# The first column pair of each MLP with seven products, its token sums made in the projection before it

## The reference

```python
def sq_relu_mlp(h, w_up, w_down):            # w_up 2048 x 8192, w_down 8192 x 2048, fp32
    return jnp.square(jax.nn.relu(h @ w_up)) @ w_down
...
h = h + sq_relu_mlp(rms_norm(h, mlp_norm_w[l]), w_up[l], w_down[l])
```

## Time and profile before

| | |
|---|---|
| median of 3 runs | 2415.95 us |
| profiled execution, device time | 2416.47 us |
| its span, first to last instruction | 2414.7 us |
| PE busy | 2404.3 us, 11523 matmuls |
| PEld / DVE / ACT / POOL busy | 2004.6 / 1935.6 / 1284.7 / 259.9 us |
| 16 DMA engines, mean | 222 GB/s |

### The profile page before, as it was taken

How to read it: one execution, slowest core, us unless ns; L and a number is a source line. 1 busy time by engine, 2 the same in 40 slices (tenths; PEclk the granted TensorE clock), 3 DMA queues, 4 the chain that set the end, 5 groups by cost and what they waited for, 6 DMA issues and landing times.

```text
span 2414.7 us, 31286 instructions
## 1 busy us (share of the span) xinstructions
PE 2404.3 (100%) x11523; PEld 2004.6 (83%) x11523; DVE 1935.6 (80%) x2107; ACT 1284.7 (53%) x1544; POOL 259.9 (11%) x394
## 2 busy tenths in 40 slices
PE   8999999999999999999999999999999999999999
PEld 7888888888888888888888888888888888888887
DVE  6788888875579889888899866566689898898897
ACT  5555565554455445455555645555555555454453
POOL 1011111111001001011011111110211010010010
PEclk9999999999999999999999999999999999999999
DMA  7777777767778668577677765655887676677684
GB/s 227 217 227 227 226 232 223 230 216 236 220 236 257 213 209 267 172 241 236 197 252 228 238 207 186 189 173 181 259 257 218 219 239 215 225 235 223 195 256 162
DMA packets 288110, 535.35 MB, mean 222 GB/s; under 512 B 22318, under 2 KB 55440, under 8 KB 286976
## 3 DMA queue, kind: packets, MB, share of 16 engines
q1 hardware_dynamic: 264736, 457.87, 59.9%
q0 software_dynamic: 22976, 75.91, 10.9%
q10 hardware_dynamic: 288, 0.11, 0.0%
HBM read 498.09 MB, written 35.72 MB: 221 GB/s over the span
## 4 chain that ended last, share of the span: by engine, by line
PE 67%; issue 25%; DMA 5%; POOL 2%; DVE 2%; ACT 0%; POOLq 0%; ACTq 0%
PE acc L515 9%; PE acc L517 9%; PE acc L516 9%; PE acc L693 7%; PE acc L695 7%; PE acc L694 7%; DMA spread<-work 4%; PE aux L515 2%; PE aux L516 2%; PE aux L517 2%; POOL work L2039 2%; PE aux L532 1%; PE aux L531 1%; PE aux L530 1%; PE aux L719 1%
## 5 line engine op out<-in xcount | busy, mean ns | idle before, releaser
L1085 ACT ACTIVATE w_hi<-w_raw 128x1024 fp32r<-128x1024 f32 x392 | 414.9, 1061 | 494.0 <-PE acc L695 379.6
L1303 DVE TENSOR_TENSOR w_lo<-w_raw,w_hi 128x1024 fp32r<-128x1024 f32 x353 | 427.8, 1221 | 236.8 <-ACT w_hi L894 236.5
L693 PE MATMUL acc<-w_hi,stationary 128*128 128x512 f32 x1564 | 609.9, 390 | 0.0
L694 PE MATMUL acc<-w_lo,stationary 128*128 128x512 f32 x1564 | 609.1, 389 | 0.0
L695 PE MATMUL acc<-w_hi,stationary 128*128 128x512 f32 x1564 | 609.1, 389 | 0.0
L1609 DVE TENSOR_TENSOR w_lo<-w_raw,w_hi 128x1024 fp32r<-128x1024 f32 x392 | 476.3, 1220 | 126.5 <-ACT w_hi L1085 121.0
L894 ACT ACTIVATE w_hi<-w_raw 128x1024 fp32r<-128x1024 f32 x353 | 370.2, 1057 | 299.2 <-PE acc L517 142.4
L515 PE MATMUL acc<-w_hi,stationary 128*128 128x512 f32 x960 | 379.8, 396 | 0.0
L517 PE MATMUL acc<-w_hi,stationary 128*128 128x512 f32 x960 | 374.4, 390 | 0.0
L516 PE MATMUL acc<-w_lo,stationary 128*128 128x512 f32 x960 | 374.2, 390 | 0.0
L693 PEld LDWEIGHTS acc<-w_hi,stationary 128*128 128x128 f32 x1564 | 293.6, 188 | 63.2 <-DVE w_lo L1609 2.9
(11 more groups left out here) (246 smaller groups left out, 2874.0 us busy)
## 6 DMA issues: line engine op xcount, KB each, us to landing
w_raw<-in_w_up SPq DMA_DIRECT2D x200, 512.0 KB
w_raw<-in_w_down SPq DMA_DIRECT2D x192, 512.0 KB
w_raw<-in_ssm_w_in SPq DMA_DIRECT2D x129, 512.0 KB
w_raw<-in_ssm_w_out SPq DMA_DIRECT2D x64, 512.0 KB
work<-in_w_down SPq DMA_DIRECT2D x64, 512.0 KB
w_raw<-in_w_kv SPq DMA_DIRECT2D x64, 512.0 KB
work<-in_w_up SPq DMA_DIRECT2D x56, 512.0 KB
spread<-work POOLq DMA_DIRECT2D x44, 512.0 KB, 4.8
```

The costliest lines, as they stand in the source:

```text
L693: pe.matmul(o, xh, hi[:, k], start=starts[t] and k == 0, stop=False)
L694: pe.matmul(o, xh, lo[:, k], start=False, stop=False)
L1085: a.activation(whi[:, unit % RING, :], raw[:, slot, :], ACT.Copy).then_inc(sem("hi_made"), 1)
L1303: v.tensor_tensor(wlo[:, s, :], raw[:, pos.raw_slot(off), :], whi[:, s, :].bitcast(F32), ALU.subtract).then_inc(sem("lo_made"), 1)
```

## The change

The first pair of each MLP becomes a form pair like the others, 19 units, with `w_up`'s quad moved from the k-tiles 12 to 15 to the k-tiles 0 to 3 (`UP_QUAD = 0`), so that the token sums come from block 0 of the residual and are made in the projection before. Its direct units go in an order that asks for the later k-tiles last (`late`). The quad's four pieces are loaded during the projection (`first_quad`). In the second pair, ACT's `fresh_relu` and DVE's `fresh_square` make way for the `add_half` and `square` of the other pairs; both halves are taken there (after units 1 and 3). The last product block of `ssm_w_out` takes its k-tiles in another order, which frees the place of the sums early. In layer 1 the PSUM banks of the forms change places, since the projection's last block stands in the other bank.

```diff
-UP_QUAD, DOWN_QUAD = 3, 0
+UP_QUAD, DOWN_QUAD = 0, 0
...
-FRESH_UNITS = ([("d", n, k) for n in (0, 1) for k in range(0, 12, 2)] + [("d", n, k) for n in (0, 1) for k in (12, 14)])
+FRESH_UNITS = pair_units(UP_QUAD, True)
...
-             + [(n, k) for n in (2, 3) for k in range(0, 32, 2)])
+             + [(2, k) for k in range(0, 32, 2)] + [(3, k % 32) for k in range(16, 48, 2)])
...
@@ SP: loads
+                if i in (56, 58, 60, 62):
+                    if i == 56:
+                        sp.wait_ge(sem("gate_lo"), GROUPS)
+                    first_quad(0, (1, 0, 3, 2)[(i - 56) // 2])
...
+                if i in (24, 26, 28, 30):
+                    if i == 24:
+                        sp.wait_ge(sem("o_ready"), 4)
+                    first_quad(1, (1, 0, 3, 2)[(i - 24) // 2])
...
@@ PE, mlp
                                 if formed(c, p) == 0:
-                                    pe.wait_ge(sem("resid_added"), R)
+                                    pe.wait_ge(sem("resid_added"), R - 1)
+                                    pe.wait_ge(sem("turned_lo"), T - 3)
+                            if what == "P7" and formed(c, p) == 0:
+                                pe.wait_ge(sem("resid_added"), R)
                             if what == "P5":
-                                if p == 1 and c == 0:
+                                if p == 0 and c == 0:
                                     pe.wait_ge(sem("sums_lo"), 5 * layer + 1)
...
@@ ACT, projections
+                if i == 57:
+                    a.wait_ge(sem("w_used"), Pos(OUT0).done(53))
+                    sums_hi(0, 0, 1, sums[1])
...
+                if i == 30:
+                    sums_hi(1, 0, 1, sums[1])
...
@@ ACT, mlp
-                                if j == 10:
+                                if j == 14:
                                     resid_hi(3, T, before)
-                                if j == 12:
-                                    sums_hi(0, 1, sums[1])
-                                continue
...
-                                if late and j in (1, 3):
-                                    fresh_relu(j // 2)
...
@@ DVE, projections
+                if i == 55:
+                    resid_sums(3, T_OUT + 1)
+                if i == 59:
+                    sums_lo(0, 0, 1, sums[1])
...
+                if i == 29:
+                    resid_sums(11, T_WO + 1)
+                if i == 31:
+                    sums_lo(1, 0, 1, sums[1])
...
@@ DVE, mlp
-                                if j == 10:
+                                if j == 14:
                                     resid_lo(3, T, before)
-                                if j == 11:
-                                    v.wait_ge(sem("turned_lo"), T)
-                                    resid_sums()
-                                if j == 13:
-                                    sums_lo(0, 1, sums[1])
-                                continue
...
                                 if late and j in (1, 3):
-                                    fresh_square(j // 2)
+                                    add_half(layer, j // 2, start - 3 + j)
+                                    square(c, j // 2)
                                     turn_up(c, j // 2)
```

117 lines of the change are left out of this document (54 added, 63 removed).

## The result

The changed kernel takes 2421.43 us in the median of 21 runs (2419.84 to 2424.35), the kernel before 2416.72 us in 21 runs beside it (2415.84 to 2418.88). The ratio is 1.0019 with a 95% interval of 1.0012 to 1.0026: slower by 4.7 us, where 3.5 were forecast, and within 0.2% of no change. The profiled execution took 2421.18 us of device time.

A forecast was written before the change was run, and what follows sets the result against it. PE, 100% busy, was taken to bound the kernel, with DVE's queue next. The terms -2.72 + 4.16 + 2.05 gave +3.49 us, 2419.4 us; range 2418.3 to 2420.9 around the forecast alone, 2415.6 to 2422.6 over all cases with exclusions.

The forecast's parts named there:

- term 2: First pair of MLP 1: DVE's chain from `w_o` makes unit 1 0.31 us and P7 1.74 us late, together +2.05 us.
- term 1: Second pair of each MLP: two added `add_half` make P7's split late, 2.08 us each, together +4.16 us.
- The saving: First pair of each MLP: twelve fewer matmuls in all at 0.2267 us each, -2.72 us.
- 1.27 us at the earliest: PE waiting for DVE: a matmul starts no sooner than 1.27 us after the start of its split.
- DVE has no pause here: Second pair of MLP 0: from the first `fresh_square` at 717.62 DVE's rows follow one another up to P7.
- DVE catches up and I count no further wait: Second pairs behind P7: one split per 2.04 us of PE at 1.13 us each, so no further wait.
- The price of `add_half`: DVE, second pairs: 1.26 us each as a dependent step; by the skill 1.13, making the whole change +2.97 us.
- the transfers in `w_o`: Bound on the sum: quad pieces loaded between the projection's pieces cost from nothing up.
- late pieces: Rival, `w_o`: quad loads delay its pieces by up to 6.2 us; half of that gives +6.6, 2422.5 us; chance 0.17.
- The first pair of MLP 0: P7's matmul at 684.14, due at 684.52: no wait, with 0.38 us to spare.
- only the second pairs wait: Rival: the chain through ACT is shorter, so MLP 1's first pair doesn't wait; +1.44, 2417.4 us; chance 0.14.
- Hidden: Rival: DVE's added work costs PE nothing, leaving only the saving; -2.72, 2413.2 us; chance 0.08.

The follow-up runs named there:

- the run with 8 columns: The changed kernel with the two added `add_half` of each second pair made on 8 of 512 columns: 2417.36 us against 2416.40, ratio 1.0001.
- the run with the second half later: The changed kernel with each second pair's second `add_half`, `square` and transpose moved from position 3 to 5, dependent work one or two positions back: 2419.44 us, ratio 1.0013.
- both queue remedies: The changed kernel with layer 1's quad loads ten pieces earlier (alone 2419.44 us) and `sums_hi` behind `resid_hi` (alone 2419.79 us); both together 2417.96 us.
- the first four experiments: Changed kernel with quad loads early, 2419.44 us; kernel before with the changed kernel's quad loads, 2417.41; changed kernel with `sums_hi` behind `resid_hi`, 2419.79; with both remedies, 2417.96.

## Why the prediction came out as it did

- **The number** lies in the whole range stated, 2415.6 to 2422.6, but 0.5 us above 2418.3 to 2420.9, the range around the forecast alone. Of the 2.0 us above 2419.4, 0.77 are the kernel before, whose median of 21 runs is higher than that of three. The other 1.2 are term 2, 1.60 too small, term 1, 0.86 too large, and the 0.5 that stands in no changed place. That two errors pull against each other is luck.
- **The saving** was right: 12 matmuls at an unchanged pitch of 0.2267 us. Every sum of the table starts from it.
- **Term 1**, the second pairs: place and mechanism were right, shown by the run with 8 columns. Its size was 2.08 us each and measured 1.65. The term that was mis-sized is the queue ahead of P7: I priced only the rows that the change adds, not the step that it alters, `fresh_square` to the transpose at 1.45 us, which became 1.26. Two of these are 0.38 of the 0.43 us; most of the rest is that the matmul starts 1.23 us after its split, which "1.27 us at the earliest" had ruled out. "DVE has no pause here" was a misreading: the trace before shows a pause of 0.23 us ahead of both transposes. "DVE catches up and I count no further wait" held only because P7's wait itself gave DVE time, as the run with the second half later shows.
- **The price of `add_half`**: 1.25 us, where the forecast had 1.26, not 1.13. The Trainium skill ("VectorE: DVE Perf Modes", The DRAIN you can't avoid) reports that a semaphore after each of a chain of copies costs nothing extra. These rows, which are other operations, disagree by 0.12 us per dependent step.
- **Term 2**, the start of MLP 1: with the pieces in time the queue's steps came out within 0.03 us. That the sum is right to the hundredth (2.05) is luck: the matmuls start 1.36 us after their splits, not 1.27, and the step behind a wait costs 0.08, not 0.11. The term was 1.6 us short since I took the lower end, nothing, for the transfers in `w_o`, and the rival *late pieces* took place in a small form, 1.6 us where it allowed up to 6.2. Its estimate of 301 GB/s when full was too low, 325 were moved. By the prediction 1.34 us of it would have made the kernel slower by over 0.2%; that term 1 was 0.86 us too large (twice 0.43) left the sum at +4.2 us, inside.
- **The first pair of MLP 0 was free**, as forecast with 0.38 us to spare: no gap there.
- The rival *only the second pairs wait* failed: it gave unit 1 and P7 of MLP 1's first pair nothing, and they waited 1.63 and 1.66 us, and still 0.37 and 1.68 with the pieces in time. *Hidden* failed in all the other places of the table.
- The Trainium skill ("DMA: Bandwidth & Descriptors", Issuing engines are not separate DMA queues) has transfers that different engines issue run on the same 16 DMA engines and interleave. The trace agrees, with a share of 1.01 and a late piece in the same stretch, and at 0.94, once the loads stood ten pieces earlier, piece 27 was in time. That POOL's round trips would slow too, as the prediction drew from it, is borne out: POOL's wait for the way out took 8.74 us in place of 5.97 for block 1 and 4.71 in place of 3.36 for block 2.

That both queue remedies act on MLP 1's first pair, and that the second pair is overfull, is shown by runs. That the remaining 0.5 us between the sum and the medians is a difference between executions is argued only; the lateness of piece 27 alone, 0.60 to 1.84 us, makes any one execution differ from the median by as much.

## What to carry to other kernels

Where the next engine is 90% busy behind a full one, follow its queue from the last row at which it stood idle to each due time, and price every step between two starts that the change alters, not only those that it adds. Before moving work to remove such a wait, count whether the whole stretch has room for it; if not, the wait reappears at the next tight unit, or at the next long latency (here a round trip of 16 to 18 us). An extra load of a few pieces was harmless where the ring covered it (1.08 us late) and cost one for one where a dependent chain started at the piece that it delayed. And look at the granted clock of every execution, not only of the profiled one.

## What the runs showed of the hardware

- A pause of TensorE can cost more than itself. Behind starts 3.03 to 3.06 us apart, in three places, the matmuls stood 0.43 us apart for 2.7 to 6.1 us, at the lower level of the clock. One such pause cost 4.3 us in one place and 5.8 in another. Behind two starts 2.5 us apart the clock stayed at 1.00 in one profiled execution, but seven other executions of that kernel had a mean clock of 0.998 or 0.999, so no safe length is shown. The kernel before, which has no such pause in its profile, shows 0.999 too in 2 of the 31 executions beside the first four experiments.
- A dependent step on DVE isn't one number: `add_half` to `square` 1.25, `square` to the transpose 1.26, `fresh_square` (which reads PSUM) to the same transpose 1.45 us. `add_half` reads PSUM too, so the source alone doesn't explain it; this stays open.
- A waiting matmul starts 1.23 to 1.37 us after the start of the 128 x 1024 split that it waits for, the same at the same place in every run: 1.23 or 1.24 at P7 of the second pairs, 1.36 or 1.37 in the first pair of MLP 1, 1.27 in the rows that the prediction read.
- Between 1698 and 1718 us, piece 27 came in time at DMA shares of 0.88 to 0.96 and 0.6 to 1.8 us late at 0.99 to 1.03 (in the changed kernel 1.6 at 1.01). On the whole it rises with the share, 0.60 at 0.99, 0.79 at 1.00, 1.08 and 1.31 at 1.02, 1.84 at 1.03; that isn't a rule, as these are single executions.
